# Griffin/NSA hybrid trunk, two layers: VectorE's order in an attention round, and coefficient transfers in pairs

## What is computed

```python
z = rmsnorm(x, g) @ w_in                      # u, g_lru, q, g_nsa, six k/v parts, gate logits
y_lru = rg_lru(causal_depthwise_conv(u))
o_cmp, p_cmp = cmp_attention(q, compress(kc), compress(vc))
o_slc = slc_attention(q_rot, rope(ks), vs, idx, ok)   # 8 blocks of 64, top 16: every causal block
o_win = win_attention(q_rot, rope(kw), vw)            # window 512: every causal key
y_nsa = gates[0]*o_cmp + gates[1]*o_slc + gates[2]*o_win
y = concatenate([y_lru * silu(g_lru), y_nsa * silu(g_nsa)])
x = x + y @ w_out
```

## Time and profile before

| what | value |
|---|---|
| runs shown | 534.31, 528.92, 528.68 us, median 528.92 |
| the profiled execution's own time | 529.5 us |
| its span, first to last instruction | 527.8 us |
| granted TensorE clock, mean | 0.997 |
| PE busy | 511.1 us (97%) |
| DVE busy | 376.4 us (71%) |
| ACT busy | 297.0 us (56%) |
| POOL busy | 79.2 us (15%) |

### The profile page before, as it was taken

One profiled execution on the slowest core, in us unless ns is written; L12 is line 12 of the kernel. 1 busy time (PEld: TensorE's weight loads), 2 busy tenths in 40 slices (PEclk: granted clock), 3 DMA queues, 4 the chain that ended last, 5 costly groups with the idle time before them and its releaser, 6 DMA issues.

```text
span 527.8 us, 8335 instructions
## 1 busy us (share of the span) xinstructions
PE 511.1 (97%) x2959; PEld 385.4 (73%) x2959; DVE 376.4 (71%) x622; ACT 297.0 (56%) x601; POOL 79.2 (15%) x141
## 2 busy tenths in 40 slices
PE   8999999999998999999999999999999899999995
PEld 7777877787775766666888687778787577676784
DVE  3686996689877687864756669668987688788432
ACT  5757636625755655663633685536365576567433
POOL 5101100121030211101440100011201122010100
PEclk9999999999999999999999999999999999999998
DMA  9878466266323434332323654934443333422014
GB/s 266 204 210 212 101 160 123 67 127 146 92 76 86 107 86 103 87 77 60 81 80 90 177 154 121 189 99 100 88 114 122 91 99 89 90 60 57 28 42 119
DMA packets 104473, 59.11 MB, mean 112 GB/s; under 512 B 43040, under 2 KB 101552, under 8 KB 104432
## 3 DMA queue, kind: packets, MB, share of 16 engines
q1 hardware_dynamic: 99232, 49.63, 37.6%
q0 software_dynamic: 3584, 7.63, 5.9%
q10 hardware_dynamic: 1616, 1.32, 0.8%
HBM read 48.31 MB, written 2.36 MB: 96 GB/s over the span
## 4 chain that ended last, share of the span: by engine, by line
PE 71%; DVE 14%; issue 4%; SPq 4%; DMA 3%; ACT 2%; POOL 1%; POOLq 0%; DVEq 0%; ACTq 0%
PE z_ps L1641 12%; PE z_ps L1643 11%; PE z_ps L1642 11%; PE o_ps L1776 4%; PE t_ps L1744 4%; PE o_ps L1641 3%; PE s_ps L1721 3%; PE o_ps L1643 3%; PE o_ps L1642 3%; PE z_ps L1721 3%; PE a_ps L1776 2%; DVE w_lo L1242 2%; DVE probs L1413 2%; DVE E L1291 1%; DMA swp<-E 1%
## 5 line engine op out<-in xcount | busy, mean ns | idle before, releaser
L1641 PE MATMUL z_ps<-h_hi,w_hi 128*128 128x512 f32 x248 | 100.6, 406 | 3.7 <-DVE E L1291 3.7
L1643 PE MATMUL z_ps<-h_hi,w_lo 128*128 128x512 f32 x248 | 96.9, 391 | 0.0
L1642 PE MATMUL z_ps<-h_lo,w_hi 128*128 128x512 f32 x248 | 96.7, 390 | 0.0
L1001 ACT ACTIVATE w_hi<-stage 128x1024 fp32r<-128x1024 f32 x54 | 57.2, 1059 | 52.1 <-PE z_ps L1643 27.9
L1242 DVE TENSOR_TENSOR w_lo<-stage,w_hi 128x1024 fp32r<-128x1024 f32 x54 | 65.8, 1219 | 7.4 <-ACT w_hi L1001 6.8
L1187 ACT ACTIVATE probsT<-t_ps 128x512 f32<-128x512 f32 (+1 forms) x62 | 37.0, 596 | 43.4 <-PE t_ps L1744 35.0
L1641 PEld LDWEIGHTS z_ps<-h_hi,w_hi 128*128 128x128 f32 x248 | 46.6, 188 | 18.1 <-issue 7.5
L1643 PEld LDWEIGHTS z_ps<-h_hi,w_lo 128*128 128x128 f32 x248 | 46.6, 188 | 10.2
L1642 PEld LDWEIGHTS z_ps<-h_lo,w_hi 128*128 128x128 f32 x248 | 46.7, 188 | 8.7 <-issue 0.2
L965 POOL DMA_DIRECT2D swp<-E x48 | 24.1, 508 | 176.5 <-DVE E L1288 102.8
L1179 ACT ACTIVATE probs<-s_ps,mn 128x128 f32<-128x128 f32 (+3 forms) x64 | 33.1, 526 | 21.6 <-DVE mn L1529 21.4
(11 more groups left out here) (272 smaller groups left out, 1058.4 us busy)
## 6 DMA issues: line engine op xcount, KB each, us to landing
stage<-in_w_in SPq DMA_DIRECT2D x27, 512.0 KB, 4.6
stage<-in_w_in SPq DMA_DIRECT2D x34, 256.0 KB, 3.9
probsT<-swp SPq DMA_DIRECT2D x72, 64.0 KB, 2.1
stage<-in_cmp_k_w SPq DMA_DIRECT2D x8, 512.0 KB, 4.0
stage<-in_cmp_v_w SPq DMA_DIRECT2D x8, 512.0 KB, 4.3
stage<-in_w_out SPq DMA_DIRECT2D x8, 512.0 KB, 3.5
stage<-in_w_out SPq DMA_DIRECT2D x16, 256.0 KB, 4.1
swp<-E POOLq DMA_DIRECT2D x48, 64.0 KB, 2.3
```

The source lines that it names most:

```text
L1001: act.activation(split_into(n)[0], stage_of(key), ACT.Copy).then_inc(hi_split, 1)
L1641: pe.matmul(bank, w_hi[:, slot, at:at + P], x_hi, start=first, stop=False)
L1642: pe.matmul(bank, w_hi[:, slot, at:at + P], x_lo, start=False, stop=False)
L1643: ins = pe.matmul(bank, w_lo[:, slot, at:at + P], x_hi, start=False, stop=last)
```

## The change

- The steps' list: SG moves from behind the second T to behind the minima and exponentials of a round, and is added there from the same list `silus`, which by then holds the chunk that `close()` has just added. TANH stays where it was.
- K of rounds 3, 5, 7 and 9 moves to the same place, behind SG. K of round 11 moves ahead of that round's O. In round 1 K stays.
- K is split into K (VectorE's operations, and GpSimd's write to DRAM) and a new step KR (GpSimd's wait for that write and the read). Where a round has two groups both K come first, then both KR.
- Of the groups that end in rounds 4, 6 and 8 (LATE_O) the second one's O, that is of (1,1), (2,2) and (3,2), comes one round later, in rounds 6, 8 and 10.

```diff
+LATE_O = (4, 6, 8)
...
+    def spread(groups):
+
+        add(*(("K", *group) for group in groups), *(("KR", *group) for group in groups))
+
+    owed = [[], []]
     fill(2)
...
             if at == 0:
                 if late:
                     add(late)
-                add(*(("O", *group) for group in ended(n - 1)))
-                if n == 1:
-                    add(*(("K", *group) for group in COEFS_AT[n]))
+                if n in (1, len(SETS) - 1):
+                    spread(COEFS_AT[n])
+                add(*(("O", *group) for group in owed[0]))
+                owed = [owed[1]]
+                second = ended(n)[1:] if n in LATE_O else []
+                owed += [[group for group in ended(n) if group not in second], second]
+                owed[0] = owed[0] + owed[1]
+                owed = [owed[0], owed[2]]
             if at == min(1, len(turns) - 1):
                 add(*tanhs)
                 if n < len(SETS) and SETS[n][0] in FAR:
                     add(("D", SETS[n][0]))
-                if n > 1:
-                    add(*(("K", *group) for group in COEFS_AT.get(n, ())))
-                add(*silus)
-                tanhs, silus = [], []
+                if n == 1:
+                    add(*silus)
+                    silus = []
+                tanhs = []
...
             add(("S", b), ("MX", b, 0), ("MX", b, 1), exps(a, 0), exps(a, 1), exps(b, 0))
+            add(*silus)
+            if 1 < n < len(SETS) - 1:
+                spread(COEFS_AT.get(n, ()))
+            silus = []
             late = exps(b, 1)
...
                     pool.dma_start(coef_rows[b].rearrange("h (a q) -> a h q", a=4), coef_t[:, b, :]).then_inc(coef_out[b], 16)
+                elif kind == "KR":
+                    _, l, i, b = st
+                    n = plan.coef_no[(l, i, b)]
                     if i >= 1:
                         pool.wait_ge(o_done, group_no[(l, i - 1, b)] + 1)
```

## The result

The changed kernel takes 542.07 us (median of 4 runs, 540.97 to 543.73), the kernel before took 528.83 beside it: ratio 1.024, 95% interval 1.0205 to 1.0273. The profiled execution took 542.0, with a span of 540.3, 12.5 more than before. Silu products are now line 1411 (they were 1393), the tanh 1104 (1086), minima 1547 (1529), an output product 1583 to 1590 (1565 to 1572), evictions 1309 (1291), the addition to x 1604 (1586), a piece 1659 (1641), W 1794 (1776).

The account below looks back on a forecast made before the run. TensorE, busy 97%, was taken to bound the kernel, with VectorE close behind. Silu stalls of +9.3 less 0.8 for round 11 gave +8.5 on 529.5, so 538.0; the median lies 0.6 lower: 537.5, range 532.5 to 543.5.

Parts of the forecast that it names:

- signs: Silu products idling 3 us and longer, six times; waits at lines 1291 and 1586 from 5.6 to some 14; W waiting.
- sign of being wrong: Silu products without idling, idling with TensorE's waits as before, or a granted clock under 1.00 inside the attention rounds.
- What bounds the kernel: TensorE, busy 97%; in the attention rounds VectorE stands so close behind that a late VectorE is seen at once.
- The pairs: GpSimd's second write no longer behind the first read: second group's coefficients some 3 us sooner, round 2's 4.72 us stall shrinks.
- The silu products: VectorE stops at SG until the next round's tanh, delaying the minima and eviction: six stalls, sum +9.3 us.
- six terms: Silu stalls, layers 0 and 1: round 2 +1.9, +2.0; round 3 +1.2, +0.2; gate chunk 3 +2.8, +1.2 us.
- Where TensorE pays: TensorE's waits for evictions (line 1291) and line 1586 grow from 5.6 to some 14 us; W waits for VectorE's O.
- Coefficients behind the minima: Rounds 5, 7, 9 and layer 1's round 3: taken at 0 for both, bounds 0 and +1.5 us each.
- Rival (d): Coefficients late in layer 1 stop O of (1,0) and W of (2,0): another 2 to 3 us, 540; chance 0.10.
- The second output product later: Rounds 5, 7, 9 relieved by 1.3, 0.6, 0.6 us, rounds 6, 8, 10 loaded: value 0, bounds −0.3 and +1.
- Round 11: Last coefficients start 0.8 us sooner, ahead of O: gain 0.8 in layer 0 only, output chunk's stall to about 0.5.
- rival (c): TensorE's clock falls in a stall, round 5's 2.8 us at that edge: taken as +4, 541.5; chance 0.10.

Follow-up runs that it names:

- a round later: Changed kernel with each silu product held one round more, behind the minima of the round in which its tanh has been issued: 523.62 us, ratio 0.988.
- silu products back: Changed kernel with only the silu products put back behind the second transposed tile, next to their tanh: 524.36 us, ratio 0.989.
- silu products alone: Kernel before with only the silu products moved behind the minima, as in the change: 545.70 us, ratio 1.029.
- fourth chunk taken back: Changed kernel with only the fourth gate chunk's silu product at its old place, the others still moved: 534.11 us, ratio 1.008.
- both edits: Changed kernel with layer 1 round 4's block transfer ahead of the w_out load, and coefficient steps ahead of the silu products: 538.41 us, ratio 1.018.

## Why the prediction was right, and where it was short

Forecast 537.5, range 532.5 to 543.5; measured 542.07. Direction and mechanism held; 4.6 us are missing, and the time lies near the upper end of the range. Of the signs, five silu products wait 3 us and longer as forecast, the sixth 2.71; and one sign of being wrong came up beside them, a granted clock under 1.00 in an attention round.

- **What bounds the kernel**: held. VectorE is busy as before and TensorE's span grew by what VectorE's idling made it wait.
- **The pairs**: held. The stall would shrink "by that much", some 3 us; it shrank by 4.5, to 0.24, and alone gave 3.8 us where "the 1.50 us of TensorE in round 2 of layer 0 and its counterpart in layer 1" had it at most at 3.0.
- **The silu products, "the step that decides"**: the mechanism is shown by three kernels (back, alone, a round later). Its six terms, forecast and increment: round 2 of layer 0 1.9 and 2.15, round 2 of layer 1 2.0 and 2.3, round 3 1.2 and 1.15, its counterpart 0.2 and 0.27, round 5 of layer 0 2.8 and 3.1, round 4 of layer 1 1.2 and 1.36. The sum is 10.3 for 9.3. Five of the six came out 0.07 to 0.3 above the forecast. In round 2 the minima begin 167.55 − 162.60 = 4.95 us after the tanh's end, for the 4.66 of the sum. Of these 0.29 us, 0.22 are the output product of (0,0): the next one starts 0.82 us after it, where it had been priced at 0.60, like a simple eviction:

```profile
164.37 0.68 DVE L1583 TENSOR_TENSOR E<-o_ps,upad 128x512 f32<-128x512 f32 x1
165.19 0.69 DVE L1589 TENSOR_TENSOR probsT<-a_ps,probsT 128x512 f32<-128x512 f32 x1
```

- **Where TensorE pays**: half right in the names. W waiting for VectorE's O was among the signs, but without a size. I looked for the wait at the evictions of line 1291 and at line 1586, and expected those rows to grow from 5.6 to some 14. They went down to 4.2, and W waiting for the output products has 8.5. The sum of both is 12.7, near the 14, because W stands earlier in TensorE's order than the piece: it takes the wait first, and the piece finds only the rest. The prediction said of W that it has to wait "for less than the eviction, which covers it"; the time is the same, the row is another.
- **Coefficients behind the minima**, taken at 0 with bounds 0 and +1.5 each: this is the term that was mis-sized most, +1.6 in round 5 of layer 1. The place was named ("O of (1,0) in round 5 may wait a little, where TensorE has no need of it yet"), and the second half of that sentence failed: the product waited 3.08 us, and ended (456.50) when TensorE was already through with its scores. What ended TensorE's wait, though, was the block transfer, late beside reads and a load at the same place. I had no price for transfers that meet. Rival (d) had this place and 2 to 3 us for it; it came in with 1.6.
- **The second output product later**, taken at 0 with bounds −0.3 and +1: alone it gave 0.8, half a microsecond beyond the lower bound. What it is worth inside the changed kernel was not measured by itself.
- **Round 11**, −0.8: half. The coefficients' first step stands 0.85 earlier against its neighbours. But write to read took 3.87 us for 3.40 (240.54 to 244.41, before 233.96 to 237.36), so the piece came 0.4 earlier, and its wait is still 1.26 where "about 0.5 us" was forecast. (That row names ScalarE's split of the weights, which ended at 252.22, at about the same time as the addition to x.) Why the write took longer here isn't shown. With the silu products back, write to read took 3.41 (230.43 to 233.84) and the wait was 0.18.
- **The clock**, rival (c), at 0.10: it came true in the stall of round 5 for which it was worked out, and cost little. The time near 541.5, which (c) gave, is no support for it. From W to the next score tiles it took 7.32 us (194.89 to 202.21), and 6.59 in the kernel with the coefficient steps ahead of the silu product, where the clock stayed (194.13 to 200.72): 0.7 us, not the 4 assumed.
- **0.5 us** stood there before the attention began. The first piece of the attention began between 142.70 and 144.00 in the kernels tried here, though none of them touches what precedes it, so I take this for the spread of single executions.

By cause: silu terms 1.0 too small, the late transfer 1.6, the clock 0.5, round 11 0.4, the start 0.5. Together that is the 4.0 by which the increments (12.5) exceed the forecast's 8.5; the rest of the 4.6 is that the changed kernel's median is 0.1 above its profiled execution, where the one of before was 0.6 below.

Nearly all these misses point the same way, so no luck of cancelling errors helped; the 0.5 of the start is chance, and the range held because its upper end allowed for late coefficients and for a fall of the clock. The forecast was a sum over stalls found one by one, and two of the misses are of things that meet (a read, a load and a transfer; a stall and the clock). What stays open is how the three transfers share the engines, and why the clock falls at one stall and not at its twin.

## What to carry to other kernels

An engine works its list in order, so a step is only as early as its latest input: before moving a step ahead of others, ask which instruction of the other engine it needs and where that one stands, and price everything queued behind it. When VectorE is close behind TensorE, read the cost at the first TensorE instruction that needs anything from behind the wait, and look at what is queued between. And judge parts together: here the moved coefficients cost 8.2 us without the pairs and nothing that was seen with them, and one wrong place cost 17.7 us and hid a gain of 4.65.

## What the runs showed of the hardware

**The clock does not follow the stall alone.** Six kernels have the same stalls of 1.75 and 0.47 us in round 2 of both layers. In layer 0 the granted clock stayed at 1.00 in three of them and fell to 0.50 in the other three (silu products alone, fourth chunk taken back, both edits); in layer 1 it stayed in four and fell in two. In the kernel with the fourth chunk taken back it fell in layer 0 and stayed in layer 1, in one execution. With the fall the four matmuls of W took 1.97 us for 1.08 in the kernel with both edits (at 166.28). And yet it cost nothing there: from that W to the score tiles of round 3 it took 7.50 us (166.28 to 173.78), and 7.52 in the changed kernel without a fall (166.75 to 174.27), since TensorE had to wait for VectorE in between and the slower matmuls filled the wait. In round 5, where TensorE had work enough, the fall cost 0.7 us, and 1.75 in the kernel with both edits, where the lower level lasted longer (194.38 to 202.72, 8.34 us). The Trainium skill ("TensorE: Matmul & The Clock Gate", Part 1: The HAM clock gate) says that the clock is set by a monitor whose watching runs free, without a new start when a kernel starts, so that the moment of a change varies with where the work lands. These traces agree as far as they go, with one sequence and two outcomes; that this is the reason no run here shows.

**Transfers that meet.** Issues of DMAs in layer 1, before (430 to 448 us), with KB each and median us from issue to landing:

```profile
probsT<-swp SPq DMA_DIRECT2D x12, 64.0 KB, 2.5
```

and after (446 to 458 us):

```profile
probsT<-swp SPq DMA_DIRECT2D x4, 64.0 KB, 5.3
probsT<-coef_rows POOLq DMA_DIRECT2D x2, 128.0 KB, 5.5
```

The blocks took twice as long with a load and coefficient reads issued within 2.4 us of them. The Trainium skill ("DMA: Bandwidth & Descriptors", Issuing engines are not separate DMA queues) says that transfers of all issuing engines run on the same 16 DMA engines and interleave. The windows above agree: the share reached 1.0 to 1.06 with GpSimd's and SyncE's transfers together.

**A write and its read through DRAM cost GpSimd some 2 to 4 us of waiting.** In round 3 of the kernel with the coefficients behind the minima the first group's read waited 2.09 us for its write, and the second group's, whose write stood behind the first read, 3.89 (178.08 and 183.92). In round 1 of the kernel before it was the other way round, 2.67 for the first (at 152.66) and 2.36 for the second. So a write behind a read isn't always slower to be ready; what is always paid in that order is a second wait in a row. With both writes first the second read had no wait at all in layer 0, and the second group's product came at 157.58 and no longer at 161.94, which is most of what the pairs gave.
